# Recurrent mixer's inputs taken from unscaled H, with 1/rms of both norms multiplied in behind the projections

## What is computed

```python
# end of the first block
h = h + ffn
return _rmsnorm(h, norm_final_w)            # x * rsqrt(mean(x*x) + 1e-6) * w
# start of the second
h = _rmsnorm_2(x, norm_mix[0])
q, f, i, g = jnp.split(h @ w_in, 4, axis=-1)            # w_in 1024 x 4096
forget = lb + (1.0 - lb) * sigmoid(f)                    # key_in = 1 - forget
o = _chunk_gated_recurrence(silu(q), key_in, i, log(forget))
o = _rmsnorm_2(o, out_norm) * silu(g)
x = x + o @ w_out
```

## Time and profile before

| what | value |
|---|---|
| median of 3 runs | 1569.65 us |
| the profiled execution's own time | 1579.08 us |
| its span | 1577.8 us |
| mean granted TensorE clock | 0.943 |
| busy share PE / DVE / ACT | 91% / 54% / 44% |
| chain that ended last: PE, DMA, ACT, DVE | 68%, 21%, 4%, 4% |
| experts end (last down projection) | about 885.7 us |
| first k projection matmul | 900.4 us |
| end of the last g tile | about 1046 us |

### The profile page before, as it was taken

One profiled execution on the slowest core, in us unless ns is written; L12 is line 12 of the kernel. 1 busy time (PEld: TensorE's weight loads), 2 busy tenths in 40 slices (PEclk: granted clock), 3 DMA queues, 4 the chain that ended last, 5 costly groups with the idle time before them and its releaser, 6 DMA issues.

```text
span 1577.8 us, 27528 instructions
## 1 busy us (share of the span) xinstructions
PE 1438.9 (91%) x11669; PEld 1213.7 (77%) x11669; DVE 859.9 (54%) x1531; ACT 688.8 (44%) x1192; POOL 10.6 (1%) x10
## 2 busy tenths in 40 slices
PE   7999999999999878878777789999999998899998
PEld 7999899899965434434343489989999986799997
DVE  5776462575522212111111458857888867678876
ACT  6443544553432111111111577555556566555553
POOL 1000000000000000000000100000000000000000
PEclk9999999999979988898978799989999998999999
DMA  7454354478889999999999554225555531445552
GB/s 235 156 163 144 127 161 134 161 246 289 341 354 420 419 420 417 420 420 419 421 420 420 202 175 134 86 75 173 175 203 193 172 121 54 134 161 199 194 176 100
DMA packets 173713, 372.05 MB, mean 236 GB/s; under 512 B 6912, under 2 KB 141184, under 8 KB 149008
## 3 DMA queue, kind: packets, MB, share of 16 engines
q1 hardware_dynamic: 173584, 370.21, 63.7%
HBM read 369.14 MB, written 1.05 MB: 235 GB/s over the span
## 4 chain that ended last, share of the span: by engine, by line
PE 68%; DMA 21%; ACT 4%; DVE 4%; issue 1%; SPq 1%; DVEq 0%; ACTq 0%
PE bank L583 18%; PE bank L585 17%; PE bank L584 17%; DMA wu<-in_expert_w_down_dram 11%; DMA wu<-in_expert_w_up_dram 9%; PE bank L1702 3%; PE bank L814 3%; PE bank L1674 2%; PE bank L1740 2%; ACT hi L536 1%; DVE lo L547 1%; PE bank L1755 1%; PE bank L948 1%; DMA raw<-in_w_in_dram 1%; PE bank L923 1%
## 5 line engine op out<-in xcount | busy, mean ns | idle before, releaser
L547 DVE TENSOR_TENSOR lo<-raw,hi 128x1024 fp32r<-128x1024 f32 (+2 forms) x315 | 375.8, 1216 | 201.1 <-ACT hi L536 200.1
L583 PE MATMUL bank<-XH,hi 128*128 128x256 f32 x1416 | 405.9, 287 | 2.5 <-ACT hi L536 1.1
L584 PE MATMUL bank<-XL,hi 128*128 128x256 f32 x1416 | 400.9, 283 | 0.0
L585 PE MATMUL bank<-XH,lo 128*128 128x256 f32 x1416 | 400.7, 283 | 0.0
L536 ACT ACTIVATE hi<-raw 128x1024 fp32r<-128x1024 f32 (+2 forms) x315 | 321.2, 1050 | 118.0 <-PE bank L585 37.0
L583 PEld LDWEIGHTS bank<-XH,hi 128*128 128x128 f32 x1416 | 271.9, 192 | 10.1 <-issue 6.7
L584 PEld LDWEIGHTS bank<-XL,hi 128*128 128x128 f32 x1416 | 271.8, 192 | 0.8
L585 PEld LDWEIGHTS bank<-XH,lo 128*128 128x128 f32 x1416 | 271.5, 192 | 0.0
L1702 PE MATMUL bank<-wu,xg 128*32 128x256 f32 x2048 | 180.6, 459 | 49.4 <-DMA wu<-in_expert_w_up_dram 44.3
L1702 PEld LDWEIGHTS bank<-wu,xg 128*32 128x32 f32 x2048 | 74.8, 127 | 128.4 <-DMA wu<-in_expert_w_up_dram 61.5
L1740 PE MATMUL bank<-wu,hidT 128*32 128x256 f32 x1024 | 74.6, 409 | 31.8 <-DMA wu<-in_expert_w_down_dram 26.5
(11 more groups left out here) (363 smaller groups left out, 2235.2 us busy)
## 6 DMA issues: line engine op xcount, KB each, us to landing
wu<-in_expert_w_gate_dram SPq DMA_DIRECT2D x64, 1024.0 KB, 27.1
wu<-in_expert_w_up_dram SPq DMA_DIRECT2D x64, 1024.0 KB, 26.9
wu<-in_expert_w_down_dram SPq DMA_DIRECT2D x64, 1024.0 KB, 27.3
raw<-in_w_in_dram SPq DMA_DIRECT2D x44, 1024.0 KB, 5.1
raw<-in_ffn_w_up_dram SPq DMA_DIRECT2D x44, 1024.0 KB, 5.0
raw<-in_ffn_w_down_dram SPq DMA_DIRECT2D x22, 1024.0 KB, 5.1
raw<-in_hgrn_w_in_dram SPq DMA_DIRECT2D x16, 1024.0 KB, 5.4
raw<-in_w_branch_ret_dram SPq DMA_DIRECT2D x8, 1024.0 KB, 7.0
```

Source lines behind the costliest of these rows:

```text
L547: dve.tensor_tensor(lo_of(u), v, hi_of(u), ALU.subtract).then_inc(*WL.inc(u))
L583: pe.matmul(dst, first[0], first[1], start=start, stop=False)
L584: pe.matmul(dst, second[0], second[1], start=False, stop=False)
L585: return pe.matmul(dst, third[0], third[1], start=False, stop=stop)
```

## The change

The last four sums are made in the order n = 0, 2, 1, 3, each into a bank of its own (4, 7, 6, 5), and two pieces of H (its left 512 columns) are turned between the third and the fourth. XH and XL come from the turned, unscaled H times the product of both norms' column weights (`w_two`). What is left of the norms, one number per token, is multiplied in after the projection: for k, q and g by DVE out of PSUM with a row broadcast over the partitions (`rsb3`, made by `pe_rows` behind tile 1), for v by ACT as a per-partition scale. ACT's Sigmoid and Silu then work on what DVE has written, and ACT no longer evacuates g. The product `gained` and its squares move behind the turning. Tile 0 goes to banks 0 and 3, with its k steps cut in two halves around the turning of the right 512 columns. The first two weight tiles are now requested ahead of `wrow`.

```diff
+    w_two = st[:, 56:64]
...
-    xs3 = at(m.place, [P, 2, D], F32, "xs3")
+    junk3 = at(m.place, [P, 8, 512], F32, "junk3")
...
+    rsb3, diag3 = at(low, [P, T], F32, "rsb3"), at(low + 1024, [P, 2, P], F32, "diag3")
...
+            if p_ == NE // 4 - 1 and j is not None:
+                return (4, 7, 6, 5)[j]
...
-            combine(NE // 4 - 1)
+            combine(NE // 4 - 1, (0, 2, 1))
+            pe_last_piece(0)
+            pe_last_piece(1)
+            combine(NE // 4 - 1, (3,))
...
-            combine(NE // 4 - 1, LAST)
+            for n in (0, 2, 1):
+                dve_sum(NE // 4 - 1, n)
...
+        LAST_BANK = (1, 2, 4, 6)
+
+        def pe_last_piece(p):
+            b = bank[LAST_BANK[p]]
...
+            for t in range(2):
+                pe.wait_ge(*MOE.dve.got("H", NE // 4 - 1, 2 * t + p // 2))
+            for j in range(2):
+                for t in range(2):
+                    k = 2 * p + j
+                    done = pe.transpose(b.ap[:, j * T + t * P:j * T + t * P + P], H[:, t, k * P:(k + 1) * P], ident)
...
+        def act_last_piece(p):
+            act.wait_ge(*LB.dve.got("w_two"))
+            act.wait_ge(*NORM.pe.got(3, "t", 2 * p))
+            for j in range(2):
+                k = 2 * p + j
+                act.activation(XH[:, k, :], b_[LAST_BANK[p]][:, j * T:(j + 1) * T], ACT.Copy,
+                               scale=w_two[:, k:k + 1]).then_inc(*NORM.act.inc(3, "h", k))
...
         def act_last_norm():
             S = LAST
-            act_split(N1 + 1)
+            act_split(N1 + 2)
...
+            for t, j in ((0, 0), (1, 0)):
+                act.wait_ge(*MOE.dve.got("H", NE // 4 - 1, 2 * t + j))
+                squares("h", H, t, j, 16 + 2 * t + j)
+            act_last_piece(0)
+            act_last_piece(1)
+            for t, j in ((0, 1), (1, 1)):
+                act.wait_ge(*MOE.dve.got("H", NE // 4 - 1, 2 * t + j))
+                squares("h", H, t, j, 16 + 2 * t + j)
+            act_last_piece(2)
+            act_last_piece(3)
+            act_split(N1 + 4)
...
         def dve_last_norm():
             S = LAST
+            dve_split(N1 + 1)
+            dve.wait_ge(*LB.dve.got("w_two"))
+            dve_last_piece(0)
+            dve_last_piece(1)
+            dve_sum(NE // 4 - 1, 3)
+            dve_split(N1 + 2)
+            dve_last_piece(2)
+            dve_last_piece(3)
+            dve_split(N1 + 3)
+            dve.wait_ge(*LD["wrow"].got())
+            for t in range(2):
+                for j in range(2):
+                    dve.wait_ge(*MOE.dve.got("H", NE // 4 - 1, 2 * t + j))
+                    dve.tensor_tensor(gained[:, t, 512 * j:512 * j + 512], H[:, t, 512 * j:512 * j + 512], wrow[:, 512 * j:512 * j + 512],
+                                      ALU.mult).then_inc(*S.dve.inc("G", t, j))
...
+            dve_split(N1 + 4)
...
+            for t in range(2):
+                dve.tensor_scalar(diag3[:, t, :], ident, st[:, t:t + 1], None, ALU.mult).then_inc(*NORM.dve.inc(3, "diag", t))
...
+            sp_tile()
+            sp_tile()
             sp.wait_ge(*MOE.pe.got("x", NE // 2 - 1, 1))
             sp.dma_start(wrow[:, :], io["prm2"]).then_inc(*LD["wrow"].inc(by=16))
...
-                pe_tile(unit2(t), 2, t % 4, 8, XH, XL, x, [(HG.act, (name, j))], sides)
+                if t:
+                    pe_tile(unit2(t), 2, t % 4, 8, XH, XL, x, [(HG.dve, (name, j))], sides)
+                else:
+                    first()
+                if t == 1:
+                    pe_rows(3, diag3)
...
-            act.wait_ge(*LAST.dve.got("r"))
-            act_norm_out(3, xs3, gained, "norm_mix_2", 0, None)
-            act_split(N1 + 2)
             act_first_out()
...
+            def gate(dst, func, name, j):
+                act.wait_ge(*HG.dve.got(name, j))
+                act.activation(dst[:, 2 * j:2 * j + 2, :], dst[:, 2 * j:2 * j + 2, :], func).then_inc(*HG.act.inc(name, j))
 
             for t, (name, j) in enumerate(kq_tiles):
                 act_tile(unit2(t), 2, AHEAD, sides)
-                keep(t, k_ if name == "k" else q_, ACT.Sigmoid if name == "k" else ACT.Silu, name, j)
+                gate(k_ if name == "k" else q_, ACT.Sigmoid if name == "k" else ACT.Silu, name, j)
...
-                keep(12 + i, g_, ACT.Copy, "g", i)
...
+            def scaled(t, dst, name, j):
+
+                dve.wait_ge(*WU.got(unit2(t) + 1))
+                dve.wait_ge(*NORM.dve.got(3, "rsb"))
+                dve.wait_ge(*LAST.act.got("H", 1))
...
+                dve.tensor_tensor(dst[:, 2 * j:2 * j + 2, :], b_[t % 4].rearrange("p (h n) -> p h n", h=2),
+                                  rsb3[:, :].rearrange("p (h n) -> p h n", h=1).to_broadcast([P, 2, T]), ALU.mult).then_inc(*HG.dve.inc(name, j))
+
+            for t, (name, j) in enumerate(kq_tiles):
                 dve_tile(unit2(t), 2, AHEAD, sides)
+                if t == 0:
+                    dve.wait_ge(*NORM.pe.got(3, "rows"))
+                    dve.tensor_copy(rsb3[:, :], b_[4][:, 0:T]).then_inc(*NORM.dve.inc(3, "rsb"))
+                scaled(t, k_ if name == "k" else q_, name, j)
...
                 dve_tile(unit2(12 + i), 2, AHEAD, sides, True)
+                scaled(12 + i, g_, "g", i)
```

More of the change, by code:

```diff
@@ L724, in pe_turns, with pe_rows @@
                 yield
-        def pe_rows(i):
+        def pe_rows(i, dg):
             b = bank[4]
@@ L1744, in down, with combine @@
                 b.taken = [(M.act, ("out", e, 1)), (M.dve, ("out", e, 3))]
-            def combine(p_):
+            def combine(p_, pieces=range(4)):
                 pe.wait_ge(*M.act.got("sw", p_))
@@ L1749, in combine @@
                 pe.wait_ge(*M.dve.got("out", 4 * p_ + 3, 3))
[L1750 to L1757, removed]
+                for n in pieces:
+                    t_, j, b = n // 2, n % 2, bank[c_bank(p_, n)]
+                    for s, key in b.taken:
+                        pe.wait_ge(*s.got(*key))
+                    pe.matmul(b.ap[:, :], sw[:, t_ * P:t_ * P + P], outp[:, 512 * j:512 * j + 512], start=True,
+                              stop=True).then_inc(*M.pe.inc("sum", p_, n))
+                    b.taken = [(M.dve, ("H", p_, n))]
             pe_gather(0, 0)
@@ L1853, in down, with combine @@
                     dve.tensor_copy(outp[32 * i:32 * i + 32, 256 * j:256 * j + 256], b_[3][32 * j:32 * j + 32, 0:256]).then_inc(*M.dve.inc("out", e, j))
[L1855 to L1868, removed]
+            def combine(p_):
+                for n in range(4):
+                    dve_sum(p_, n)
             dve.wait_ge(*ROUTE.act.got("uP", 1, 1))
@@ L2186, in pe_hgrn, with first @@
             x = normed(3)
-            pe_norm(3, xs3)
             sides = [pe_hgrn_heads(0), pe_hgrn_heads(1)]
-            for t, (name, j) in enumerate(kq_tiles):
-                pe_tile(unit2(t), 2, t % 4, 8, XH, XL, x, [(HG.act, (name, j))], sides)
+            def first():
+                for b in (bank[0], bank[3]):
+                    for s, key in b.taken:
+                        pe.wait_ge(*s.got(*key))
+                    b.taken = [(HG.dve, ("k", 0))]
+                for part in (range(4), range(4, 8)):
+                    for j in range(2):
+                        u = unit2(0) + j
+                        pe.wait_ge(*WH.got(u))
+                        pe.wait_ge(*WL.got(u))
+                        for k in part:
+                            for s, key in x(k):
+                                pe.wait_ge(*s.got(*key))
+                            done = three(b_[3 * j][:, 0:T], hi_of(u)[:, k, :], lo_of(u)[:, k, :], XH[:, k, :], XL[:, k, :],
+                                         False, k == 0, k == 7)
+                        if k == 7:
+                            done.then_inc(*WU.inc(u))
+                        elif j == 0:
+                            pe_last_piece(2)
+                            pe_last_piece(3)
+                step(*sides)
+                step(*sides)
+            for t, (name, j) in enumerate(kq_tiles):
+                if t:
[4 more added lines that the diff above has]
+                    pe_rows(3, diag3)
             for i in range(4):
```

56 lines of the change are left out of this document (36 added, 20 removed).

## The result

The changed kernel takes 1577.53 us (median of 7 runs, 1575.04 to 1581.98); the kernel before, run beside it, takes 1570.0 us (7 runs, 1568.01 to 1573.23). The ratio is 1.0049, with a 95% interval of 1.0032 to 1.0066: slower by 7.7 us (5.0 to 10.4). The profiled execution of the changed kernel has 1581.98 us, a span of 1580.7 us and a mean clock of 0.956.

What follows compares the result with a forecast made beforehand. The prediction took a loop of ACT and DVE to set the end from 904 to 976 us. Its terms, -1.9 + 11.65 - 0.2 - 1.65 = +7.9, put 1569.65 at 1577.5 us, with an 8-in-10 range of 1564.5 to 1583.

Steps and rivals of the forecast that it cites:

- Front: Last sums to hi(8): PE's unit 3 ends 5.7 us earlier, but only 1.9 us of that is left at hi(8).
- Loop: Tiles 2 to 7, hi(8) to lo(20): gates waiting for DVE's scaled rows lose 3.85, 1.7 and 6.1 us, together 11.65.
- the ring: Closed ACT-DVE cycle in the loop: scaled row, gate, next hi, then DVE's lo, each waiting for the other; adds 11.65 us.
- The block behind it: PE's work from the double scores at 976.7 on moves as one block with DVE's arrival, 9.5 us later.
- the 0.2 of slack: At the first double scores DVE's copies were 0.2 us ahead of PE, so 0.2 us comes off the delay.
- Tail: Stage's end: last g evacuation and table load leave ACT's list, so the spread L978 starts earlier, -1.65 us.
- Sum: Whole kernel: -1.9 + 11.65 - 0.2 - 1.65 = +7.9 us.
- (a): Rival, loop: scaled and gate fit into time ACT and DVE wait anyway, so faster, 1562 to 1565 us; chance 0.20.
- (b): Rival, loop: part of the work lay on DVE's free time, so no difference, 1565 to 1574 us; chance 0.17.
- (c): Rival, v tiles: PE's longer waits bring the lower clock there, +2 to +5 us, 1580 to 1583; chance 0.15.

Runs made afterwards that it cites:

- Experiment 3: Changed kernel without the row multiplication of k, q and g and its broadcast row, ACT evacuating those banks as before: 1563.86 us, ratio 0.9956 to the kernel before.
- experiment 5: Kernel before, with g of the last column tiles copied out of its banks by DVE in place of ACT: 1571.6 us, ratio 0.9985.
- experiment 2: Kernel before; for k and q DVE copies the bank to SBUF and ACT's Sigmoid or Silu waits for that copy: 1588.13 us, ratio 1.0114.
- experiment 1: Changed kernel, ACT's gate of each tile moved behind the high part of the next tile's first unit: 1568.31 us, ratio 0.9978 to the kernel before.
- experiment 4: Changed kernel, row multiplication of tiles 1 to 7 made twice, the gate waiting for the second: 1581.88 us, ratio 1.0074 to the kernel before.

## Why the prediction held

The predicted 1577.5 us is the measured median, and that is better than its steps deserve: the time of the stage was right, and two things that it left out cancelled.

- **Front.** The first product starts at 886.05 + 7.44 = 893.5 (predicted 894.2); unit 3 waits for lo(3) and its products end near 900.3 + 7.44 = 907.7 (907.6); PE then waits 2.2 us for lo(4) (2.5). hi(8) starts 910.60 - 879.34 = 31.26 us after the first of the last sums, before 919.87 - 886.78 = 33.09: 1.83 us left of the front (1.9). Of ACT's waits for the DMA only one of 0.8 us is left, ahead of all this. Experiment 3 shows 5.3 of the 5.7 us as real. That each time fits so well is partly luck: with a clock of 1.00 in the sums, as in the two moved copies of the changed kernel, hi(8) comes at 29.8 us. But before, it varies too, with its waits for the DMA (33.09, 32.44 and 31.74 in three profiles), and at 96 bytes the two kernels differ by 1.9 us again.
- **Loop.** From hi(8) to lo(12) 17.45 us (17.2). The tiles behind it, from lo(12) to lo(20), 9.26, 10.06, 14.74 and 11.33 us (9.15, 9.95, 14.6, 11.25). From hi(8) to lo(20) that is 62.84 against 50.50 before: +12.3, where the prediction has +11.65. The scaled row lasts 0.68 us, against the 0.65 taken; the ring's other steps make the remaining few tenths.
- **The block behind it.** The first scores stand at 935.05 + 7.44 = 942.5 behind a wait of 9.74 us (942.1, nearly 10), lo(20) at 973.44 + 7.44 = 980.9 (980.1). The first double scores start 979.82 - 879.34 = 100.48 us after the first of the last sums, before 976.74 - 886.78 = 89.96: +10.5 (+9.5). The term of the loop was 0.7 us too small, and the 0.2 of slack did not show.
- **Tail.** Root at 1047.88 and 1050.21, spread at 1051.64: from the double scores 71.82 us, before 73.64: -1.82 (-1.65). Another 0.5 us is gained up to the first product of the output projection, which I had not counted. A table load lasts 1.28 us in these rows too and the next ACTIVATE starts at once (1046.59 and 1047.88; 1050.69 and 1051.99). The Trainium skill, page "ScalarE: Activation LUTs", section "What ACT_TABLE_LOAD costs", has a drain of about the same length besides; the trace doesn't show one, and experiment 5 gives the 1.8 of the rows, not the 3 that the page's figure would.
- **Sum.** 10.5 - 1.8 - 0.5 = +8.2 in the stage, against +7.9.
- **Missed: the place of the tiles.** The prediction prices the 8 columns of `norm_fin` at nothing, in that it doesn't speak of them. They move the expert weights by 32 bytes, and this place gives 4.7 us back (0.30% in the kernel before moved by 32). Against it the change costs at equal place 9.3 us at 96 bytes (the standard error of 1.3 doesn't exclude the 7.9 forecast) and 12.4 at 32 (9 to 16 by the two intervals). The place and this excess nearly cancel, so the total agreed to the last digits by luck, the stage by its own working. Where the excess over the stage's 8.2 us comes from stays open; in the pair at 96 bytes the start is 1.4 us longer, the rest 3.4 longer and the experts 1.7 shorter. The forecast for the profiled execution, 1587.0, was 5.0 too high: the experts of this pair took 6.4 us less and the start 1.1 less, while the rest took 2.2 more, and none of the three was in the sum.
- **Rivals.** (a) and (b) are refuted by the waits of the gates, by experiment 2 and by experiment 1: with the ring open the change gains, -3.5 us, so that rival's price was right for another order of the same instructions. (c), the clock, did not happen where it would cost: the second low stretch (957.3 to 963.3) lies where the ring is the bound, and that tile's 14.74 us is as forecast. Its mechanism is real one step further: in experiments 2 and 4 the low stretch reaches the v tiles and costs 1.6 and 2.8 us. Ahead of those two stretches PE stood 2.44 and 3.03 us for the copies. By the Trainium skill, page "TensorE: Matmul & The Clock Gate", section "HAM oscillation — how this bites in real kernels", work that is cut up by waits for operands comes back to the low clock again and again: these two agree. The changed kernel stood 2.43, 2.43 and 2.45 us at the same place in its three profiles and kept 1.00, so behind a wait of this length it can go either way, and what decides was not found.

## What to carry to other kernels

When the evacuation of a bank is handed from one engine to another in two steps, look at what stands behind the second step in an in-order list: here the instruction behind it was the one that feeds the first engine, and a row of 0.68 us cost 1.8 us in tile 4 (9.26 against 7.45) until one split was moved ahead of it (7.45 again in experiment 1). A gain at the front of such a loop arrives only as far as the loop's first late link lets it (1.8 of 5.7 us with the ring, 5.3 without). And before a difference of some tenths of a per cent is put down to the change, compare stages that it doesn't touch, and run the kernel before with its tiles moved as the change moves them.

## What was not expected of the hardware

The rate of a stream of 1 MB loads into fixed tiles was 420 or 425 GB/s by where the tiles lie, steps of 32 bytes apart (0: 420, 32: 425, 64: 419, 96: 420), 5.6 us over the 201 MB of expert weights as an estimate from the two rates. Moved by 96 bytes, the kernel before is 0.26% (0.11 to 0.41) faster at an unchanged rate, its start 3.4 us shorter in the profile; whether that is the place or the execution wasn't tried.

The clock behind waits of nearly the same length. PE's timeline and windows around the first double scores, of the changed kernel:

```profile
979.82 3.81 PE L816 MATMUL bank<-t,t 128*128 128x128 f32 x32 [2.43 <-DVE t L878]
```

```profile
981.00:982.00 1.00, 1.00 (x11) 1.00 (x10) 1.00 (x2) 0.87 (x1) 0.00 (x0) 1.00 0.05 16
```

and of experiment 2:

```profile
985.12 5.10 PE L814 MATMUL bank<-t,t 128*128 128x128 f32 x29 [2.44 <-DVE t L876]
```

```profile
986.00:987.00 1.00, 1.00 (x7) 1.00 (x7) 1.00 (x2) 0.93 (x1) 0.00 (x0) 0.50 0.08 19
```

The same stand of 2.4 us, then 11 products in a microsecond in the one and 7 in the other. The two moved copies of the changed kernel (2.43 and 2.45 us) kept 1.00 as well, experiment 4 (3.03 us) fell to 0.50. What tells them apart wasn't tried.
